# A diffusion backbone in split fp32: which engine accumulates the modulation units in the feed-forwards

## The reference, cut to what matters

```python
silu_c = jax.nn.silu(c)
m = jnp.split((silu_c @ w_mod[i] + b_mod[i])[:, None, :], 9, axis=-1)   # i: layer
h = h + 0.5 * m[2] * swiglu(modulate(rms_norm(h), m[0], m[1]), w_ff_in[i, 0], w_ff_out[i, 0])
h = h + m[5] * mixer(modulate(rms_norm(h), m[3], m[4]))
h = h + 0.5 * m[8] * swiglu(modulate(rms_norm(h), m[6], m[7]), w_ff_in[i, 1], w_ff_out[i, 1])
```

## Time and profile before

| | |
|---|---|
| the three runs | 1920.15 to 1921.01 us, median 1920.53 |
| profiled execution | 1920.4 us, of which the span is 1918.4 |
| PE busy | 1835.3 us (96%), 8540 instructions |
| DVE busy | 1201.6 us (63%) |
| ACT busy | 621.6 us (32%) |
| POOL busy | 161.9 us (8%), 145 instructions |

### The profile page before, as it was taken

The page is one execution under the profiler, slowest core; times in us unless marked ns, Lnnn a source line. Parts: engine busy times, 40 slices in busy tenths (PEclk is TensorE's granted clock), DMA queues, the critical chain, the costliest instruction groups (busy, mean ns, idle before and its releaser), DMA issues.

```text
span 1918.4 us, 21832 instructions
## 1 busy us (share of the span) xinstructions
PE 1835.3 (96%) x8540; PEld 1501.2 (78%) x8540; DVE 1201.6 (63%) x1531; ACT 621.6 (32%) x787; POOL 161.9 (8%) x145
## 2 busy tenths in 40 slices
PE   5899999999999999999999999999996899999999
PEld 2688888877897888888878888888772698888888
DVE  6867676675367767676876674447688464545354
ACT  2432322233243222223432222225775442222221
POOL 0000000020020000000200000002883110000000
PEclk8999999999999999999999999999997899999999
DMA  8844435250135535444246351311120223232301
GB/s 292 276 160 161 168 133 195 110 175 1 53 125 174 208 121 179 149 151 178 94 171 218 110 175 66 132 67 45 45 88 0 88 80 118 88 109 73 124 22 66
DMA packets 160542, 239.18 MB, mean 125 GB/s; under 512 B 3821, under 2 KB 110525, under 8 KB 160220
## 3 DMA queue, kind: packets, MB, share of 16 engines
q1 hardware_dynamic: 160160, 238.04, 35.7%
q10 hardware_dynamic: 316, 0.23, 0.0%
HBM read 236.16 MB, written 2.10 MB: 124 GB/s over the span
## 4 chain that ended last, share of the span: by engine, by line
PE 79%; DVE 11%; POOL 3%; ACT 3%; issue 2%; DMA 1%; SPq 0%; POOLq 0%; DVEq 0%; ACTq 0%
PE bank L1530 14%; PE bank L1532 14%; PE bank L1537 14%; PE bank L1423 10%; PE bank L1424 10%; PE bank L1425 10%; DVE bank L1376 3%; POOL tmp_c L579 2%; DVE mod_acc L937 2%; DVE w_lo L914 2%; DMA raw_pair<-in_w_mod 1%; PE bank L1504 1%; PE bank L1499 1%; PE bank L1497 1%; POOL sq_sum L544 1%
## 5 line engine op out<-in xcount | busy, mean ns | idle before, releaser
L1530 PE MATMUL bank<-a_hi,w_hi 128*128 128x512 f32 x1408 | 552.8, 393 | 4.7 <-ACT a_hi L627 4.7
L1532 PE MATMUL bank<-a_hi,w_lo 128*128 128x512 f32 x1408 | 549.8, 390 | 0.0
L1537 PE MATMUL bank<-a_lo,w_hi 128*128 128x512 f32 x1408 | 435.3, 391 | 1.3 <-DVE a_lo L1009 1.3
L1530 PEld LDWEIGHTS bank<-a_hi,w_hi 128*128 128x128 f32 x1408 | 265.6, 189 | 62.0 <-issue 6.3
L1124 DVE SCALAR_TENSOR_TENSOR h<-bank,half_gate,h 128x512 f32<-128x512 f32 x320 | 233.6, 746 | 122.5 <-PE bank L1425 121.8
L1537 PEld LDWEIGHTS bank<-a_lo,w_hi 128*128 128x128 f32 x1408 | 265.2, 188 | 57.7 <-DVE a_lo L1009 2.4
L1532 PEld LDWEIGHTS bank<-a_hi,w_lo 128*128 128x128 f32 x1408 | 265.5, 189 | 56.4 <-issue 1.4
L1423 PE MATMUL bank<-p_hi,w_hi 128*128 128x512 f32 (+1 forms) x768 | 287.6, 374 | 6.6 <-DVE h L1131 3.8
L1424 PE MATMUL bank<-p_hi,w_lo 128*128 128x512 f32 (+1 forms) x768 | 286.0, 372 | 0.0
L1425 PE MATMUL bank<-p_lo,w_hi 128*128 128x512 f32 (+1 forms) x768 | 285.9, 372 | 0.0
L914 DVE TENSOR_TENSOR w_lo<-raw_pair,w_hi 128x2048 fp32r<-128x2048 f32 x106 | 245.1, 2313 | 62.8 <-ACT w_hi L735 47.9
(11 more groups left out here) (163 smaller groups left out, 1864.1 us busy)
## 6 DMA issues: line engine op xcount, KB each, us to landing
raw_pair<-in_w_ff_in SPq DMA_DIRECT2D x88, 1024.0 KB, 7.1
raw_mod<-in_w_mod SPq DMA_DIRECT2D x66, 1024.0 KB, 8.1
raw_down<-in_w_ff_out SPq DMA_DIRECT2D x44, 1024.0 KB, 8.6
raw_pair<-in_conv_w_in SPq DMA_DIRECT2D x8, 1024.0 KB, 6.9
raw_pair<-in_w_mod SPq DMA_DIRECT2D x6, 1024.0 KB, 15.4
raw_pair<-in_fnet_w_out SPq DMA_DIRECT2D x4, 1024.0 KB, 6.6
raw_pair<-in_conv_w_out SPq DMA_DIRECT2D x4, 1024.0 KB, 6.3
raw_mod<-in_x SPq DMA_DIRECT2D x4, 512.0 KB, 5.4
```

The source lines that it names most:

```text
L1530: pe.matmul(ps[banks + s][:], tile_hi, a_hi[:, k], start=k == 0, stop=False, skip_group_check=True)
L1532: pe.matmul(ps[banks + s][:], tile_lo, a_hi[:, k], start=False, stop=False, skip_group_check=True)
L1537: ins = pe.matmul(ps[banks + s][:], w_hi[b][:, s * KD + k], a_lo[:, k], start=False, stop=k == KD - 1, skip_group_check=True)
```

## The change

`mod_mac` and `mod_lo` of the 32 units of the feed-forwards are taken off VectorE. GpSimd gets `mod_unit`, called for a whole feed-forward at a time by `ff_units(f)`, between its additions of squares. GpSimd has no fused step here, so each row block is a multiplication into one of two term buffers (`mod_term`, which lie in u_pad) and an addition into mod_acc, and GpSimd also does the subtraction for the low part. The four units at the beginning stay on VectorE. TensorE gets a wait ahead of output chunk d = 2 of step 1 in feed-forwards 0 and 1 for the columns of `mod_columns` (the transposed rows lie in the bank of that chunk), which the order on VectorE ensured before.

```diff
+        mod_term = u_pad[:, 0:2, HALO:HALO + T]
...
+        s_mod_term = sem("mod_term_ready")
...
+            def mod_unit(unit):
+
+                loads = unit * 16 + 16 * (3 - HEAD)
+
+                def term(j):
+                    if j % 4 == 0:
+                        pool.wait_ge(s_mod_in[j // 4], loads)
+                    if j >= 3:
+
+                        pool.wait_ge(s_mod_mac, unit * 8 + j - 1)
+                    pool.tensor_scalar(mod_term[:, j % 2], raw_mod[:, j // 4, j % 4], silu_c[:, j:j + 1], None,
+                                       ALU.mult).then_inc(s_mod_term, 1)
+
+                pool.wait_ge(s_mod_in[0], loads)
+                pool.wait_ge(s_mod_split, unit)
+                pool.tensor_scalar(mod_acc[:], raw_mod[:, 0, 0], silu_c[:, 0:1], None,
+                                   ALU.mult).then_inc(s_mod_mac, 1)
+                term(1)
+                for j in range(1, KD):
+                    if j + 1 < KD:
+                        term(j + 1)
+
+                    pool.wait_ge(s_mod_term, unit * 7 + j - 14)
+                    pool.wait_ge(s_mod_mac, unit * 8 + j)
+                    pool.tensor_tensor(mod_acc[:], mod_acc[:], mod_term[:, j % 2], ALU.add).then_inc(s_mod_mac, 1)
+                pool.wait_ge(s_mod_hi, unit + 1)
+
+                pool.wait_ge(s_mod_sum, unit)
+                pool.tensor_tensor(mod_acc_lo[:], mod_acc[:], mod_acc_hi[:].bitcast(F32),
+                                   ALU.subtract).then_inc(s_mod_split, 1)
+
+            def ff_units(f):
+                first = FF_UNIT0[f] - 2
+                for unit in range(first, first + UNIT_STEPS[f] + 2):
+                    mod_unit(unit)
+
+            ff_units(0)
             ff_square_adds(1)
             project_square_adds(2)
+            ff_units(1)
             ff_square_adds(3)
+            ff_units(2)
             ff_square_adds(4)
...
-                if unit is not None:
-                    mod_mac(unit, mod_half_ready(i * 16 + 16 * (FF_UNIT0[f] - HEAD + 2)), ring_rows)
-                if unit is not None and after_down is not None:
-                    mod_lo(unit)
                 gated(f, i, 0, par)
...
-                if unit is not None and after_down is None:
-                    mod_lo(unit)
                 gated(f, i, 1, par)
...
-                if u0 is not None:
-                    ring_mac(u0)
                 gate_product(f, 0, 0)
                 next_lo(f, 0, 0, 0)
-                if u0 is not None:
-                    mod_lo(u0 - 2)
                 product_lo(f, 0, 0, 0)
-                if u0 is not None:
-                    mod_mac(u0 - 1, mod_half_ready(16 * (u0 + 2 - HEAD)), ring_rows)
                 gated(f, 0, 1, 0)
                 next_lo(f, 0, 1, 0)
                 if u0 is not None:
                     mod_row(u0 - 2)
-                    mod_lo(u0 - 1)
...
-            def down(f, done, par, unit):
+            def down(f, done, par, unit, columns=None):
...
+                    if d == 2 and columns is not None:
+
+                        pe.wait_ge(s_mod, columns)
...
-                    down(f, i - 1, 1 - par, unit)
+                    down(f, i - 1, 1 - par, unit, GATE_MOD[f] if late_unit and f < 2 else None)
```

More of the change, by code:

```diff
@@ L944, in mod_lo @@
                                   ALU.subtract).then_inc(s_mod_split, 1)
[L946 to L952, removed]
             def mod_row(unit):
@@ L976, in row_range_columns @@
                 dve.tensor_tensor(cols[0], src, cols[1], ALU.add).then_inc(s_mod, 1)
-            def ring_mac(unit):
-                mod_mac(unit - 2, mod_half_ready(16 * (unit - HEAD + 1)), ring_rows)
             def square_add(n, o):
```

## The result

| | before | after |
|---|---|---|
| median of the runs, us | 1920.63 (1920.15 to 1921.01, 4 runs) | 1999.20 (1995.24 to 2000.52, 4 runs) |
| profiled execution, us | 1920.4 | 2000.45 |
| its span, us | 1918.4 | 1998.5 |

The change makes the kernel slower: ratio 1.0406, 95% interval 1.0388 to 1.0424, 78.6 us by the medians. The forecast was 1976.5 us in a range from 1946 to 2005. Sign and place were right, the size was too small: 79 us lost where 56 were forecast.

What follows compares the result with a forecast made beforehand. TensorE, busy 96% of the span, was taken as the bound, with gaps only at feed-forward starts. Fourth chunks 16.4, 18.4 and 21.4 us late, body 0, make 56 us on 1920.4: 1976.5 us, range 1946 to 2005.

Steps and rivals of the forecast that it cites:

- The body: Later steps of the feed-forwards: a GpSimd unit takes 21.4 us and stays hidden with 8 us to spare, cost 0.
- The row update's thin cover: Body steps: 1.0 us of cover before TensorE needs the row; a GpSimd instruction may delay it 0 to 0.3 us, 0 taken.
- The place of the waits: TensorE waits at each feed-forward's start, for the accumulator's low half twice and the row once, and never in the body.
- From S to the fourth chunk: Each feed-forward's start: units two and three in series on GpSimd, then the tail to TensorE's fourth output chunk, 49.6 us.
- S: End of the first unit's subtraction in each feed-forward, forecast at 74, 583.1 and 965.8 us.
- M: Time of one unit's eight multiplies and seven adds on GpSimd, taken as 15.5 us, ends 14.1 and 20.1.
- the prediction's own sign: In the profile after, a GpSimd multiply outside 0.5 to 1.3 us would show the forecast wrong; 0.70 was taken.
- The norm's part: Second and third feed-forwards' norms: GpSimd's first unit holds up VectorE's instructions with two SBUF inputs, 3 us each.
- The clock: Starts: longer TensorE waits may lower its clock, but slow matmuls mostly lie under the next wait; 0 taken, up to 2 us each.
- The cheap GpSimd: Rival for the starts: multiply at 0.52 us and neither engine holding the other up, 1944 us, as a mixture to 1962; chance 0.22.
- the body caught: Rival: a body unit takes more than its 29 us, each microsecond over paid in 23 steps, 2 us over giving 2023; chance 0.05.
- The dear GpSimd: Rival for the starts: multiply at 1.27 us, 2004 us, up to 2015 with a late first unit and clock losses; chance 0.12.

Runs made afterwards that it cites:

- body_only: The changed kernel with units one to three of each feed-forward back on VectorE, only the 23 later ones on GpSimd: 1920.35 us against 1919.87 before, ratio 1.0003.
- starts_only: The changed kernel with only the first three units of each feed-forward on GpSimd, the 23 others back on VectorE: 1998.52 us, ratio 1.0413.
- terms_by_memset: The changed kernel with seven of each unit's eight GpSimd multiplies replaced by memsets of the same width, products left out: 1956.40 us, ratio 1.0195.

## Why the forecast was right in place and short in size

**The body (cost 0): right.** Both bounds hold in the trace and in body_only. The unit that begins behind step 2's subtraction (159.40 in after, where 132.6 and the 26.8 us of the first start give 159.4) ends at 184.21, after 24.8 us instead of 21.4, and ScalarE copies it at 188.80, when its own work has come that far. 4.6 us of cover are left where 8 were forecast. The row update's thin cover was enough: no matmul of the body waits for it.

**The place of the waits: right.** The low half twice and the row once at each start, none in the body. The forecast's list left out one wait that before has too, the transposition's for the row: 2.5 us in each of the first two starts. starts_only shows the whole loss.

**From S to the fourth chunk: the term that failed.** It was to take 49.6 us and takes 57.9 in each start (76.12 to 133.98, 608.31 to 666.26, 1015.79 to 1073.68). By its parts, in the second start:

| part | forecast | measured | from |
|---|---|---|---|
| unit two | M + 3.3 = 18.8 | 23.96 | S to the copy at 632.27 |
| copy and subtraction | 2.1 | 1.98 | 632.27 to 634.25 |
| unit three | M + 2.2 = 17.7 | 22.53 | 634.25 to 656.78 |
| copy to fourth chunk | 11.0 | 9.48 | 656.78 to 666.26 |
| sum | 49.6 | 57.95 | |

M was taken as 15.5 us, with an upper end of 20.1, and is 21.1. Eight multiplies at 1.53 instead of 0.70 us are 6.6 us more, seven adds at some 1.27 instead of 1.42 are 1.0 less. By the prediction's own sign, a multiply outside 0.5 to 1.3 us, this step was wrong. The failed step is the bound "above: the two-input add, 1.27 us". That a one-input instruction costs no more than one with two inputs of the same width was an assumption without a row. The select of the earlier trace rows, 0.29 us for a quarter of the width, drew the choice to the lower end, though it is a different operation.
The Trainium skill (GPSIMD Engine Reference, 4.1 Engine selection) has one-input elementwise work on GpSimd roughly at line rate. The trace disagrees: 1.56 us, where VectorE took 0.48 for the same scaling in before (line 932), and where on GpSimd a memset of the same tile takes 0.53 and the two-input product 1.04. By the 769 ns that section 3.1 of that page gives for a tight loop over 512 elements, the estimate for the total would be 1980, 19 us short.

**The smaller terms** took back part of it. The disturbances of units two and three were 2.8 and 1.4 us instead of 3.3 and 2.2. The 1.5 us added to the tail for collisions of VectorE with the next unit never appeared: 9.48, 9.48 and 9.49 us, against 9.5 in the earlier trace rows. In sum 2.9 us a start came back.

**S, the end of the first unit: right within 2.1 us.** In the first start 76.1 (forecast 74). In the second 608.31 less the 25.15 us by which that stretch begins late is 583.2 (forecast 583.1). In the third 1015.79 less 52.1 is 963.7 (forecast 965.8). The norm's part was forecast at 3 us in both: 3.2 and 0.5 were measured.

**The sum.** Per start the chain adds 8.3 us, S adds 2.1, 0.1 and -2.1. Between the first and the second feed-forward 1.6 us came back: in the mixing stage before has TensorE at half clock twice (matmuls 0.427 us apart, from 438.5 to 441.0 and from 444.9 to 447.9), the profiled execution of after only the first time, though for longer (from 464.5 to 468.7); where before has the second stretch, it has full clock (0.227 apart), and a wait 0.8 us shorter just ahead. So 56.2 + 3 x 8.3 + 0.1 - 1.6 = 79.6, and 79.7 was measured.

That 1999.2 lies inside the range of 1946 to 2005 is in part luck. With M at its measured 21.1 us and all else as forecast, the sum is 1976.5 + 6 x 5.6 = 2010 us, outside the range. The overestimated smaller terms and the 1.6 us of the mixing stage, 10 us together, brought it back.

**The clock (0 taken): right, for the reason given.** After each long wait the chip granted TensorE half clock, the 1.2 GHz level, for 3.4 to 4.7 us. Three lines of after show the end of one such stretch in the third start: 0.43 us from the first to the second, 0.35 to the third, and 0.22 to 0.24 from matmul to matmul behind them:

```profile
1069.28 0.63 PE L1441 MATMUL bank<-p_lo,w_hi 128*128 128x512 f32 x1
1069.71 0.51 PE L1439 MATMUL bank<-p_hi,w_hi 128*128 128x512 f32 x1
1070.06 0.39 PE L1440 MATMUL bank<-p_hi,w_lo 128*128 128x512 f32 x1
```

It made the matmuls 13.4 us longer in sum, yet the fourth chunk still waits for the row for 0.39 to 0.93 us in every start, so the slow matmuls lay under waits that were there anyway.

**VectorE's busy time** was to fall by 206 us and fell by 164. Of the missing 42 us some 36 stand in groups of VectorE whose instructions got longer while GpSimd works beside them: the low part of the down weights alone, 45 times 2.70 instead of 2.29 us, is 18.6. The rest is not assigned.

**The rivals.** The cheap GpSimd (0.22) and the body caught (0.05) were wrong by the rows above. The dear GpSimd (0.12), 2004 to 2015 by a multiply of 1.27 us and further losses, was right in its mechanism: the multiply was dearer still, and its surcharges for the tail and the norms didn't come. terms_by_memset, with the cheap rival's price for seven of the eight multiplies, lands at 1956, not at its 1944. From S to the fourth chunk it takes the rival's 42.0 us or less (41.0 to 42.0); what the rival left out is GpSimd holding VectorE up in the norms, 5.3 and 2.6 us there.

## What to carry to other kernels

VectorE, busy for two thirds of the time, was not the bound here, and work taken from it was worth at most the waits at the ends of its chains: 11.5 us in all, and the move put 75.6 in their place. Before serial steps move to another engine, look for the stretch in which several of them are due one after the other; the period of the steady loop (33 us, and 21 to 25 needed) says nothing of it. And a price that no row shows must not be capped by the row of another operation because that one seems to do more: the upper end should have lain above it.

## What the runs showed of the hardware

- On GpSimd a product of a 128x512 tile with a column takes 1.56 us in the one-input form and 1.04 us in the two-input form with the column spread along the row. With a constant it takes 1.49 (one run), a memset 0.53, an add 1.09 to 1.30.
- The two forms differ in what they do to VectorE. Beside one-input multiplies the norm's instructions with two tiles of SBUF stay at 0.48 us, beside adds they don't (after, VectorE, then GpSimd of the same stretch):

```profile
577.41 0.48 DVE L1085 SCALAR_TENSOR_TENSOR a_lo<-tmp_b,mod,a_hi 128x256 fp32r<-128x256 f32 x1 [0.18 <-ACT a_hi L698]
...
582.57 1.11 DVE L1085 SCALAR_TENSOR_TENSOR a_lo<-tmp_b,mod,a_hi 128x256 fp32r<-128x256 f32 x1
```

```profile
576.24 3.11 POOL L571 TENSOR_SCALAR u_pad<-raw_mod,silu_c 128x512 f32<-128x512 f32 x2
...
582.03 1.37 POOL L585 TENSOR_TENSOR mod_acc<-mod_acc,u_pad 128x512 f32<-128x512 f32 x1
```

  It fits that the norms lost less than forecast, and that the faster two-input form lost more there. In the other direction there is no such difference: a 2.3 us subtraction of VectorE stretches a one-input multiply as well, from 1.56 to 5.61 us at 142.89, where two of them stand one behind the other:

```profile
142.89 5.61 POOL L571 TENSOR_SCALAR u_pad<-raw_mod,silu_c 128x512 f32<-128x512 f32 x1
```

```profile
141.75 3.19 DVE L955 TENSOR_TENSOR w_lo<-raw_pair,w_hi 128x2048 fp32r<-128x2048 f32 x1
144.86 2.28 DVE L961 TENSOR_TENSOR w_lo<-raw_down,w_hi 128x2048 fp32r<-128x2048 f32 x1
```

  The Trainium skill (SBUF — State Buffer, Who interferes with whom) has a VectorE instruction with two SBUF inputs contend with a GpSimd instruction that reads SBUF, and calls such contention an exclusive lock. The adds (0.48 us became 1.11) and the last rows agree. The multiply beside the 0.48 us instruction, which reads SBUF too, does not: both keep their time.
